# A two-stage transformer on one core: both feed-forward blocks by Strassen's scheme in fp32, with part of the weight sums on GpSimd

## The reference, cut to what matters

```
def swiglu(h, w_gate, w_up, w_down):
    return (jax.nn.silu(h @ w_gate) * (h @ w_up)) @ w_down
for l in range(2):                      # layer 0: S5 mixer, layer 1: latent attention
    shift1, scale1, gate1, shift2, scale2, gate2 = jnp.split(silu(c) @ ada_w[l] + ada_b[l], 6, axis=-1)
    ...
    x = x + gate1 * mix
    h = modulate(rms_norm(x, norm2_g[l]), shift2, scale2)
    x = x + gate2 * swiglu(h, ffn_w_gate[l], ffn_w_up[l], ffn_w_down[l])
```

## Time and profile before

| | |
|---|---|
| median of 3 runs | 1143.36 us (1142.41 to 1145.6) |
| profiled execution | 1144.42 us |
| its span, first to last instruction | 1142.6 us |
| granted clock of PE, mean | 0.991 |
| PE busy | 1077.2 us (94%) |
| DVE busy | 467.6 us (41%) |
| ACT busy | 290.3 us (25%) |
| POOL busy | 64.0 us (6%) |
| layer 0's feed-forward | 128.6 to 365.1 us |
| layer 1's feed-forward | 511.6 to 737.1 us |

### The profile page before, as it was taken

The page is one execution under the profiler, slowest core; times in us unless marked ns, Lnnn a source line. Parts: engine busy times, 40 slices in busy tenths (PEclk is TensorE's granted clock), DMA queues, the critical chain, the costliest instruction groups (busy, mean ns, idle before and its releaser), DMA issues.

```text
span 1142.6 us, 19466 instructions
## 1 busy us (share of the span) xinstructions
PE 1077.2 (94%) x8485; PEld 902.1 (79%) x8485; DVE 467.6 (41%) x928; ACT 290.3 (25%) x695; POOL 64.0 (6%) x84
## 2 busy tenths in 40 slices
PE   6879999999999999899999999999996899999997
PEld 4648888888888857588888888878886688888686
DVE  8996445444314728622000000234914561602632
ACT  6512500000002564512000000124413251202632
POOL 3010011110101000000000000000003100000000
PEclk9999999999999999999999999999999999999999
DMA  9995889899844443263535432444440003544220
GB/s 292 350 317 172 282 322 376 323 350 358 317 161 119 139 143 108 81 200 111 194 115 171 160 113 77 143 142 133 128 162 6 5 3 111 184 150 145 75 75 37
DMA packets 120271, 195.67 MB, mean 171 GB/s; under 512 B 4161, under 2 KB 103115, under 8 KB 113787
## 3 DMA queue, kind: packets, MB, share of 16 engines
q1 hardware_dynamic: 109754, 131.15, 35.8%
q0 software_dynamic: 10144, 62.92, 14.5%
q10 hardware_dynamic: 288, 0.36, 0.1%
HBM read 191.53 MB, written 1.05 MB: 169 GB/s over the span
## 4 chain that ended last, share of the span: by engine, by line
PE 81%; DVE 11%; ACT 3%; issue 3%; DMA 1%; SPq 0%; DVEq 0%; ACTq 0%
PE psum L665 59%; PE psum L1027 13%; DVE arena L1766 4%; PE psum L940 2%; PE psum L1551 1%; ACT arena L2629 1%; DVE sq L1766 1%; DVE arena L1772 1%; DVE arena L1936 1%; PE psum L1526 1%; DVE arena L2030 1%; ACT sq L2629 1%; DVE arena L1769 1%; DVE xT L1772 1%; PE psum L1675 1%
## 5 line engine op out<-in xcount | busy, mean ns | idle before, releaser
L665 PE MATMUL psum<-hT,ring 128*128 128x256 f32 x1392 | 311.4, 382 | 2.9 <-DVE hT L1772 2.0
L665 PEld LDWEIGHTS psum<-hT,ring 128*128 128x128 f32 x1392 | 263.3, 191 | 42.3 <-issue 7.2
L2629 ACT ACTIVATE arena<-psum 128x512 f32<-128x512 f32 (+6 forms) x225 | 101.5, 479 | 615.9 <-PE psum L665 568.8
L665 PE MATMUL psum<-hT,arena 128*128 128x256 f32 (+2 forms) x984 | 165.0, 339 | 4.6 <-DVE hT L1766 4.6
L665 PEld LDWEIGHTS psum<-hT,arena 128*128 128x128 f32 (+2 forms) x984 | 143.5, 181 | 24.5 <-issue 6.4
L1766 DVE TENSOR_TENSOR arena<-arena,psum 128x256 f32<-128x256 f32 (+2 forms) x76 | 39.0, 530 | 264.9 <-ACT arena L2629 235.5
L665 PE MATMUL psum<-arena 64*64 64x64 f32 (+6 forms) x2252 | 87.9, 240 | 18.7 <-issue 14.0
L665 PEld LDWEIGHTS psum<-arena 64*64 64x64 f32 (+3 forms) x2252 | 68.6, 140 | 32.2 <-issue 28.3
L1027 PE MATMUL psum<-arena,ring 128*128 128x256 f32 x384 | 85.1, 380 | 0.0
L1027 PEld LDWEIGHTS psum<-arena,ring 128*128 128x128 f32 x384 | 72.6, 190 | 11.0 <-issue 1.2
L665 PE MATMUL psum<-ring,arena 128*128 128x256 f32 (+2 forms) x288 | 73.3, 415 | 0.5 <-ACT arena L2629 0.5
(11 more groups left out here) (281 smaller groups left out, 1043.8 us busy)
## 6 DMA issues: line engine op xcount, KB each, us to landing
aring<-in_ada_w POOLq DMA_DIRECT2D x36, 1024.0 KB, 8.4
ring<-in_a_w_in SPq DMA_DIRECT2D x14, 1024.0 KB, 5.4
arena<-in_ffn_w_gate SPq DMA_DIRECT2D x12, 1024.0 KB, 7.5
arena<-in_ffn_w_up SPq DMA_DIRECT2D x12, 1024.0 KB, 7.9
ring<-in_ffn_w_down SPq DMA_DIRECT2D x12, 1024.0 KB, 5.1
ring<-in_ffn_w_gate SPq DMA_DIRECT2D x10, 1024.0 KB, 9.9
ring<-in_ffn_w_up SPq DMA_DIRECT2D x10, 1024.0 KB, 7.1
arena<-in_ffn_w_down SPq DMA_DIRECT2D x10, 1024.0 KB, 5.0
```

What stands on the lines that cost most here:

```text
L665: return eng.matmul(dst, w, x, start=first, stop=last)
L2629: return eng.activation(dst, x, f, **k)
```

## The change

Both blocks use Strassen's scheme in Winograd's form on 2x2 blocks: 7 products of half size for 8, with sums of the weights, of the activations and of the products. The first two hidden chunks are computed as before. Then ten units j = 1 to 10, each of 256 hidden columns, split the gate and up weights into halves of 512 rows, and the tokens into halves of 128. After them come the down products, in four output pairs i of 256 columns; each takes three weight panels (4, 4 and 3 pairs of hidden chunks; d = 3 i + q numbers them), now cut by output columns. All products have 128 columns (tokens).

VectorE forms the sums of activations (`combine_tokens`, `combine_hidden`), and combines the products out of PSUM. The weight sums: in layer 1 VectorE forms four per unit (1024 elements a partition each) and four per down panel (512, or 384). In layer 0 VectorE forms two per unit, and GpSimd the other two and all of the down panels'. GpSimd's modulation loads stand between these sums, in its one program. The modulation panels are used two per unit and four per output pair, instead of two per chunk (one from chunk 14 on); the rows and columns of modulation blocks 5 and 6 move into the down part. Block 6 is summed in `hT`.

The core of the diff (PE's order; VectorE's per unit; GpSimd):

```
+    for j in range(1, NDN):                                   # PE
+        ...
+        eng.wait_ge(*next_bank(p1, pool))
+        multiply(p1, g[:, lo], hT3[:, lo, 0:P]).then_inc(*pe.signals("half_products"))
+        eng.wait_ge(*summed(l, j, 2))
+        ...
+        multiply(p6, s2, t2).then_inc(*fills(p6))
+        eng.wait_ge(*summed(l, j, 3))
+        eng.wait_ge(*next_bank(p7, pool))
+        multiply(p7, u[:, lo], t3).then_inc(*pe.signals("half_products"))
+        eng.wait_ge(*next_bank(p5, pool))
+        multiply(p5, s1, t1).then_inc(*pe.signals("half_products"))
+        eng.wait_ge(done("first_copied"), copy_of(l, j))
+        multiply(p1, g[:, hi], hT3[:, hi, 0:P], False).then_inc(*fills(p1))
+        eng.wait_ge(*summed(l, j, 4))
+        eng.wait_ge(done("halves_read"), 2 * nth + 2)
+        multiply(p5, s4, hT3[:, hi, P:T], False).then_inc(*fills(p5))
+        ...
+        eng.wait_ge(done("halves_read"), 2 * nth + 1)
+        multiply(p7, u[:, hi], t4, False).then_inc(*fills(p7))
+    for i in range(KC // 2):
+        for q in range(DOWN_PANELS):
+            ...
+            if i == 0:
+                eng.wait_ge(done("tokens_combined"), 24 * HALVED.index(l) + 4 + (8, 16, 20)[q])
+            multiply(px, 0, w[:, :, 0, 0:P], hp[:, :, 0, 0:P])
+            eng.wait_ge(*down_summed(l, d))
+            multiply(px, 1, s2, t2)
+            ... (five more)
```

```
+    for j in range(1, NDN):                                   # VectorE
+        if j < NDN - 1: combine_weights(l, j + 1, 2)
+        tt(u2, ps(p6), u2, ALU.add)                           # waits first_copied (ScalarE), p6
+        if l and j < NDN - 1: combine_weights(l, j + 1, 3)    # j = 10: combine_down(l, 0)
+        tt(u3, ps(p7), u2, ALU.add)
+        tt(up[:, :, half_1], ps(p5), u3, ALU.add)
+        beside(j, False)                                      # layer 0: one modulation panel
+        if l and j < NDN - 1: combine_weights(l, j + 1, 4)    # j = 10: combine_down(l, 1)
+        if j % 2 == 0 and j < NDN - 1: combine_hidden(l, [j - 2, j - 1])
+        tt(hid[:, two, half_1], ps(p5), u2, ALU.add)
+        if j < NDN - 2: combine_weights(l, j + 2, 1)
+        tt(up[:, :, half_0], ps(p7), u2, ALU.add)
+        tt(hid[:, two, :], hid[:, two, :], up, ALU.mult)      # waits for silu (ScalarE)
+        beside(j, True)                                       # layer 0: one modulation panel
+    combine_hidden(l, [8, 9, 10])
+    # down: layer 0, per i: (bias), four modulation panels, then seven sums out of PSUM, two updates of xT3
```

```
+    ahead = EARLY + ARING                                     # GpSimd, layer 0
+    combine_beside(1)                                         # two sums of 1024
+    for j in range(1, NDN):
+        if j < NDN - 1:
+            combine_beside(j + 1)
+        for i in range(ahead, ahead + 2):
+            ada_load(i)
+        ahead += 2
+    for d in range(DOWN_PANELS * KC // 2):
+        combine_down(d)                                       # four sums of 512 or 384
+        for i in range(ahead, min(ahead + (2 if d % 3 == 1 else 1), len(ada_source))) if d > 1 else ():
+            ada_load(i)
+            ahead = i + 1
```

## The result

The changed kernel takes **1160.48 us** (median of four runs, 1159.59 to 1162.07), against 1142.9 for the kernel before on the same chip: ratio **1.015**, 95% interval [1.013, 1.017]. It is slower, by about 17 us; forecast were 1167 us and slower. The profiled execution took 1159.59 us with a span of 1157.7, 15.1 more than before.

What follows compares the result with a forecast made beforehand. PE's work (busy 94% of the span) was taken to set the time. Block A +42 and block B -18 give +24, from 1143.4 to 1167 us; range 1130 to 1186.

Steps and rivals of the forecast that it cites:

- The sign and its two causes: Whole kernel slower, chance 0.76: layer 0's block A loses 42 us, layer 1's block B gains 18 us.
- PE's own work: Both blocks: 1736 instructions of 128 columns at 0.1115 us make 193.6 us, so -20.5 us a block.
- Waits that stand alone: Both blocks: waits in front of a group cost 0.05 to 0.06 us each, +5 us a block, bounds 0 and +8.
- Block B, VectorE keeps up: Layer 1: VectorE needs 8.5 us of a 12.9 us unit, 1.3 us spare, so PE stays the bound.
- The end of the block: Layer 1, last down matmul to next stage's work: about 9 us instead of 12.4, so -3.4 us.
- Block A's units: Layer 0's gate and up: VectorE and GpSimd taking turns make a unit 14.1 us on average, bounds 12.9 and 15.
- the price list: VectorE operation times from the earlier trace, such as 1024 SBUF elements 1.22 us and a modulation panel 2.35 us.
- Block A's down part: Layer 0 from T, the down part's start (288 us): 25.7 us a pair, PE ends T+104, memory lands T+120; +43 us.
- rival 3: Layer 0's down part: PE idles and the clock falls, or landings take 10 us; pairs 29 us, 1190 us or more; chance 0.07.
- the walk through the queue: Layer 0's down part followed step by step along GpSimd's queue: panels 5, 8, 11 ready at T+49, T+75, T+100.
- (1): Layer 0: VectorE and GpSimd times do not add up, unit 12.9 us, kernel 1142 us; chance 0.15.
- (2): Layer 0's down part: sums keep ahead of PE if GpSimd never waits for a modulation panel; 1117 us; chance 0.14.

Runs made afterwards that it cites:

- Run 1: Strassen's scheme in layer 1 alone, layer 0 as before the change, against the kernel before: 1124.06 us, ratio 0.9819.
- run 4: Changed kernel, layer 0's down-part modulation sums taking their second input from idle PSUM, not SBUF (sums left out): 1146.6 us, ratio 1.0013 to the kernel before.
- run 3: Changed kernel with layer 0's down-part modulation loads issued by ScalarE instead of GpSimd: 1140.79 us, ratio 0.9964 to the kernel before.
- run 5: Changed kernel with first two down panels' sums before unit 10's loads and down-part modulation loads from ScalarE: 1138.91 us, ratio 0.9941 to the kernel before.
- run 6: Changed kernel with the edits of run 2, run 3 and run 4 together, the same sums left out: 1133.9 us, ratio 0.9922 to the kernel before.
- run 2: Changed kernel with GpSimd forming layer 0's first two down panels' sums before unit 10's modulation loads: 1155.27 us, ratio 1.0097 to the kernel before.
- run 9: Changed kernel with 34 calls of a 256-column matmul on constants before the memory's transposes: 1157.51 us, ratio 1.0109 to the kernel before.
- run 10: Changed kernel with the edits of run 2 and run 3 and 20 matmul calls on constants before the memory lands: 1134.57 us, ratio 0.9909 to the kernel before.
- run 7: Changed kernel with 68 calls of a 256-column matmul on constants before the memory lands: 1167.52 us, ratio 1.021 to the kernel before.
- run 8: Changed kernel with the edits of run 2 and run 3 and 44 matmul calls on constants: 1143.26 us, ratio 0.9994 to the kernel before.

## Why the prediction was right, point by point

The sign and its two causes held, and the time is 6.5 us below the forecast. That it comes so near is in part luck: the units of block A were taken 10.5 us too long, and the handover at the lower clock, which the sum didn't have, gives 4.2 of them back. Block A costs 37.7 us up to the start of the key-value projection (371.40 before, 409.08 after; forecast +42), block B gives back 21.6 (from 518.43 to 749.53 before, 231.1, and from 556.34 to 765.89, 209.55; forecast -18). Run 1 confirms the second by time (-20.7), and with it the first.

- **PE's own work**: taken as 0.1115 us an instruction, measured 0.1117. Right.
- **Waits that stand alone**: the step "+5 us a block" failed. B's 1736 instructions take 193.85 us with all their waits, where the forecast had 193.6 for them without any. The rows it was built on the earlier trace rows show a first group after a wait that ended late; a wait whose semaphore is already there showed no cost here.
- **Block B, VectorE keeps up**: right, PE idle 0 of 193.8 us. The end of the block was mis-sized: 8.55 us from the last down product (757.34) to 765.89 (forecast 9), but before the change it was 10.0, not 12.4. I had taken 737.10, where the chain leaves PE for VectorE, for the end of PE's products. PE's timeline before the change has them run on to 739.52:

```profile
732.61 7.07 PE L1027 MATMUL psum<-arena 128*128 128x256 f32 x32
739.52 5.03 PE L665 MATMUL psum<-aring,ring 128*128 128x256 f32 x22
```

  So -1.5 instead of -3.4.
- **Block A's units**: the step "mean 14.1 us" failed; a unit took 12.70 and PE set it. With a stall of 2.57 us at the head (forecast 2) and the rows, gate and up took 132.1 us instead of 143. The other units of A took as little, three of them 37.59 us. The turns are there: VectorE's timeline in the changed kernel has

```profile
182.99 2.13 DVE L1966 TENSOR_SCALAR sq<-aring,c_act 128x2048 f32<-128x2048 f32 x1
...
185.96 2.46 DVE L1963 TENSOR_TENSOR arena<-arena 128x1024 f32<-128x1024 f32 x1
...
195.73 3.83 DVE L1969 SCALAR_TENSOR_TENSOR sq<-aring,c_act,sq 128x2048 f32<-128x2048 f32 x1
```

  and GpSimd's beside it

```profile
181.54 5.79 POOL L3644 TENSOR_TENSOR arena<-arena 128x1024 f32<-128x1024 f32 x2
...
192.59 4.82 POOL L3644 TENSOR_TENSOR arena<-arena 128x1024 f32<-128x1024 f32 x2
```

  The first GpSimd pair ends at 187.33 and VectorE's sum 1.09 us later, though alone it takes 1.22; the second ends at 197.41 and VectorE's panel 2.15 later, alone 2.35. So 0.1 to 0.2 us of the second instruction lie beside the first, as far as the ends on GpSimd can be trusted, which the profile calls rough. By the price list the engines' times in a unit add to 13.4, as forecast; some four such changes bring it to about 12.8. The one modulation operation in eight that only multiplies saves little: it took 2.13 us beside GpSimd's sums (182.99), where alone it takes 1.28. That the sum comes down to PE's 12.7 in this way is argued, not tested by a run of its own. The Trainium skill, "SBUF — State Buffer", section "Who interferes with whom", calls the ports that the two engines share an exclusive lock, and has the other engine blocked for the whole instruction, there of VectorE's two-port modes. The rows here, of instructions with two SBUF inputs, agree but for these 0.1 to 0.2 us. The same section of the Trainium skill says that outside those modes a DVE instruction with at most one SBUF input doesn't contend, and run 4 agrees: 2.35 us inside GpSimd's 5.08.
- **Block A's down part**: right in place, cause and nearly in size. First sums T+10 (forecast 11.5); the third panels of the last three pairs (d = 5, 8 and 11) summed at T+48.5, T+74.1 and T+100.5 (forecast 49, 75 and 100); PE's end T+105.5 (104), memory landed T+121 (120), with T = 277.5 us. Both causes are shown by runs: the loads in GpSimd's queue cost 21 us (run 3), of which up to 8 can be the issuing and the rest is the order; the turns cost 15 with that order (run 4), and 2 to 6, within the noise, without it (runs 5 and 6). They overlap: mending one hides most of the other. The first sums behind the loads of unit 10 cost 6 (run 2).
- **The clock**: the prediction had it only in rival 3 and at too high a price. It is in the result: after 15.57 us of idle the handover ran with a granted clock of 0.50 and took 4.2 us more. So A's +42 became 37.7: 10.5 less up to T (277.5 for 288), 1 more from there to the landing, 4.2 more in the handover, and a rest of 1. In the down part the granted clock fell as well (0.84), which the walk through the queue left out; since GpSimd's sums ended PE's waits there, the times came out as forecast all the same.
- **The rivals**: (1) is refuted as a mechanism, since run 4 shows that the turns cost 15 us, though its unit was the right one. (2) is what run 3 made of the kernel in part: once its sums of the down part have begun, GpSimd never waits for a modulation panel, which was the condition, and the time falls by 21 us. But the price was wrong, 1140.8 us in place of 1117: in run 3's chain in order of time nearly all from 303 to 380 us is landings of panels and VectorE's work, not PE's. (3) came true in its condition, in the main (PE idle for 20 of 105.5 us and 15.5 more behind them, the clock at 0.84), but not in its price: the pairs took 25.6 and 26.5 us, not 29.

Still open: what the two slots cost. Run 6 shows the chain of landing and sum; a third slot wasn't tried.

## What to carry to other kernels

Strassen's scheme in fp32 on TensorE gives what the count of 128-column instructions says, 9% of a block here, as long as an engine with free time forms the sums. Count each engine's time for a unit, and add those of VectorE and GpSimd where VectorE's instruction has two SBUF inputs. Don't put a load that waits for another engine's progress into the queue of an engine whose sums TensorE waits for: the same loads from ScalarE's queue were worth 21 us. The gap of TensorE before the next stage cost more here than its length: matmuls on constants that end when the data lands gave back about 4 us (runs 9 and 10), and matmuls that ran on behind it cost 6 to 7 (runs 7 and 8). Count an fp32 matmul as two instructions.

## What was not expected of the hardware

A gap of 15.6 us on TensorE was followed by 10.5 us at granted clock 0.50 while it was busy for 10.54 of 10.60 us; filled with matmuls on constants, the same handover took 7.5 us (run 9), or 6.1 at 1.00 when they ran right up to it (run 7). Waits whose semaphore was already there cost nothing measurable between groups of 128-column fp32 matmuls: 0.1117 us an instruction over 1736. When VectorE and GpSimd take turns, the second instruction ends 0.1 to 0.2 us sooner after the first than its own length. VectorE's multiplication of a modulation panel by a column, with one SBUF input, took 2.13 us beside GpSimd's sums and 1.28 without them, so one input is not always enough to be undisturbed; no run here tests why.
